# Adding expert blocks' low halves by an identity product, one-step one-hots, and all low splits on DVE

## The reference

```python
q = (h @ w_q).reshape(T, 8, 256)                      # 8 heads
s1 = einsum('thd,kd->thk', q[..., :128], k1)          # 128 keys
s2 = einsum('thd,kd->thk', q[..., 128:], k2)
v1, i1 = top_k(s1, 16)
v2, i2 = top_k(s2, 16)
cand = v1[..., :, None] + v2[..., None, :]            # 256 candidates
top, pos = top_k(cand, 16)
idx = (i1 * 128 + i2) at pos                          # of 16384 experts
g = softmax(top)
act = gelu(einsum('thkd,td->thk', u_tab[idx], h)) * g
out = einsum('thk,thkd->td', act, v_tab[idx])
```

## Time and profile before

| | |
|---|---|
| median of 3 runs | 2080.0 us (2078.1 to 2082.48) |
| the profiled execution | 2074.85 us |
| its span, first to last instruction | 2073.1 us |
| mean granted TensorE clock | 0.973 |
| UP, MID, ROUTE, DOWN begin at about | 584, 775, 975, 1385 us |

### The profile page before, as it was taken

One profiled execution on the slowest core, in us unless ns is written; L12 is line 12 of the kernel. 1 busy time (PEld: TensorE's weight loads), 2 busy tenths in 40 slices (PEclk: granted clock), 3 DMA queues, 4 the chain that ended last, 5 costly groups with the idle time before them and its releaser, 6 DMA issues.

```text
span 2073.1 us, 30937 instructions
## 1 busy us (share of the span) xinstructions
PE 1853.7 (89%) x9774; PEld 1575.1 (76%) x9774; DVE 1656.0 (80%) x2537; ACT 901.2 (43%) x1399; POOL 379.9 (18%) x281
## 2 busy tenths in 40 slices
PE   4999999898999997888889888978999999999997
PEld 4888886337988886777888888876677777777675
DVE  4668887666888999999988888857777777777786
ACT  3011233106455443444666666654444444444444
POOL 0000000000013243333444344421101010101010
PEclk9999999998999999999999999999999999999999
DMA  9997665996966668777888888888898989898885
GB/s 359 422 421 268 223 233 194 395 404 243 335 229 211 211 220 305 246 240 251 307 310 311 310 311 298 304 289 322 309 338 314 338 314 333 313 335 319 325 313 204
DMA packets 135958, 618.04 MB, mean 298 GB/s; under 512 B 16049, under 2 KB 24785, under 8 KB 99025
## 3 DMA queue, kind: packets, MB, share of 16 engines
q1 hardware_dynamic: 105984, 464.57, 61.8%
q0 software_dynamic: 18496, 134.24, 17.5%
q10 hardware_dynamic: 11410, 18.36, 2.4%
HBM read 600.26 MB, written 16.79 MB: 298 GB/s over the span
## 4 chain that ended last, share of the span: by engine, by line
DVE 20%; PE 15%; DMA 15%; issue 13%; ACT 5%; POOL 1%; DVEq 1%; SPq 1%; ACTq 1%; POOLq 0%
DMA raw<-in_peer_v 11%; DVE w_lo L379 7%; PE ps L1346 5%; PE ps L998 4%; PE ps L1007 3%; ACT w_hi L720 3%; DMA raw<-in_peer_u 2%; DVE oh L1387 2%; DVE big L1427 2%; DVE big L1863 2%; PE ps L1299 1%; POOL w_lo L379 1%; DVE big L1763 1%; ACT oh L839 1%; DMA big<-in_peer_v,row_ix 1%
## 5 line engine op out<-in xcount | busy, mean ns | idle before, releaser
L720 ACT ACTIVATE w_hi<-raw 128x1024 fp32r<-128x1024 f32 x544 | 574.5, 1058 | 641.9 <-DMA raw<-in_peer_v 143.4
L379 DVE TENSOR_TENSOR w_lo<-raw,w_hi 128x1024 fp32r<-128x1024 f32 x476 | 595.5, 1257 | 231.6 <-ACT w_hi L720 209.6
L998 PE MATMUL ps<-a,w_hi 128*128 128x384 f32 x2048 | 428.0, 352 | 6.2 <-ACT w_hi L720 5.4
L1346 PE MATMUL ps<-w_hi,a 128*128 128x512 f32 x1536 | 397.2, 394 | 24.6 <-ACT w_hi L720 18.8
L998 PEld LDWEIGHTS ps<-a,w_hi 128*128 128x128 f32 x2048 | 363.8, 197 | 7.7 <-issue 6.3
L1346 PEld LDWEIGHTS ps<-w_hi,a 128*128 128x128 f32 x1536 | 286.6, 189 | 99.1 <-ACT w_hi L720 32.6
L1007 PE MATMUL ps<-a,w_lo 128*128 128x192 f32 x2048 | 286.3, 282 | 58.1 <-DVE w_lo L379 41.3
L1007 PEld LDWEIGHTS ps<-a,w_lo 128*128 128x128 f32 x2048 | 274.2, 198 | 79.4 <-DVE w_lo L379 58.5
L1346 PE MATMUL ps<-w_lo,a 128*128 128x512 f32 x1024 | 283.6, 399 | 35.2 <-DVE w_lo L379 35.1
L379 POOL TENSOR_TENSOR w_lo<-raw,w_hi 128x512 fp32r<-128x512 f32 x136 | 217.5, 1621 | 409.0 <-ACT w_hi L720 378.1
L1346 PEld LDWEIGHTS ps<-w_lo,a 128*128 128x128 f32 x1024 | 188.5, 189 | 97.9 <-DVE w_lo L379 61.0
(11 more groups left out here) (227 smaller groups left out, 1803.1 us busy)
## 6 DMA issues: line engine op xcount, KB each, us to landing
raw<-in_peer_u SPq DMA_DIRECT2D x256, 512.0 KB
raw<-in_peer_v SPq DMA_DIRECT2D x256, 512.0 KB
early<-in_w_ada SPq DMA_DIRECT2D x60, 1024.0 KB, 10.4
early<-in_w_front SPq DMA_DIRECT2D x42, 1024.0 KB, 9.5
raw<-in_w_ada SPq DMA_DIRECT2D x20, 1024.0 KB, 10.0
raw<-in_peer_wq SPq DMA_DIRECT2D x32, 512.0 KB
big<-in_w_gate_f SPq DMA_DIRECT2D x16, 1024.0 KB, 5.5
raw<-in_w_front SPq DMA_DIRECT2D x14, 1024.0 KB, 8.7
```

Of the source, the lines that this page charges most:

```text
L379: engine.tensor_tensor(w_lo[:, s % 2, part], ring[j % ph.ring][:, part], w_hi[:, s % 2, part].bitcast(F32), ALU.subtract)\
L720: act.activation(w_hi[:, s % 2, :], ring[j % ph.ring], ACT.Copy).then_inc(hi_ready, 1)
L998: done = pe.matmul(ps[:, b % 2, 0:2 * TD].rearrange("p (m t) -> p m t", m=2), w_hi[:, half, k * P:(k + 1) * P], a_pair[:, kc, :, 0:TD], st ...
L1346: done = pe.matmul(ps[:, 4 * tt + 2 * (j % 2) + n, :], a, w[:, j % 2, n * 512:(n + 1) * 512], start=i is None and blk == 0 and w is w_hi a ...
```

## The change

Columns 0 to 191 and the low half are added by PE: ACT copies the low half into a new fp32r tile `low`, and PE multiplies it by an fp32r identity into the same columns of the bank, between the two units of the next block (`add_low`). `add_block` is gone from DVE. ACT takes the gelu straight from PSUM into `stage`, and PE uses the bank again after the gelu.

A mask group is made by DVE alone: one compare for the four plain one-hots and, for each token, one instruction with two scalar operands that compares and multiplies by the gate. ACT's scaling is gone. Two of the six groups of an iteration (all of them in ROUTE's first) are made a unit earlier.

All units are of kind "w": DVE makes every low part and POOL none. The pairs of 256-column pick instructions become single instructions of 512 columns. At DOWN's start the first sums of rows begin at unit 6 and not before unit 2; the small matrix `pair` takes over the space of `sel_T` and is made there.

```diff
 PH_WQ = Phase(None, BLOCKS // 4, "wwwwwwww")
-PH_UP = Phase(PH_WQ, EXPERT_BLOCKS // 32, "wwwp" * 4)
-PH_MID = Phase(PH_UP, EXPERT_BLOCKS // 32, "wwpwwpwwpwwpwwpw")
-PH_ROUTE = Phase(PH_MID, EXPERT_BLOCKS // 16, "wwwp" * 4)
+PH_UP = Phase(PH_WQ, EXPERT_BLOCKS // 32, "w" * 16)
+PH_MID = Phase(PH_UP, EXPERT_BLOCKS // 32, "w" * 16)
+PH_ROUTE = Phase(PH_MID, EXPERT_BLOCKS // 16, "w" * 16)
 PH_DOWN = Phase(PH_ROUTE, EXPERT_BLOCKS // 8, "w" * 16)
...
 ROWS = PEER_HEADS * TOPK // SLICES
-USE_FIRST, MASK_FIRST, PUT_FIRST = (5, 7, 9, 11, 13, 15), (5, 7, 9, 11, 13, 15), (7, 9, 11, 13, 15, 15)
-USE, MASK, PUT = (1, 4, 6, 9, 12, 14), (0, 3, 6, 8, 11, 14), (3, 6, 8, 11, 14, 15)
+USE_FIRST, MASK_FIRST, PUT_FIRST = (5, 7, 9, 11, 13, 15), (4, 6, 8, 10, 12, 14), (7, 9, 11, 13, 15, 15)
+USE, MASK, PUT = (1, 4, 6, 9, 12, 14), (0, 3, 5, 8, 11, 13), (3, 6, 8, 11, 14, 15)
 DOTS_MID_FIRST, DOTS_MID = tuple(range(6, 16)), (1, 4, 6, 9, 12, 14)
...
 assert ROW_ROUTE + N_ROUTE * (PH_ROUTE.n - 1) == ROWS and N_MID % 3 == 0 and N_ROUTE % 3 == 0
-SUMS_AT = (0, 2, 4, 6, 8, 10, 12, 14)
+SUMS_FIRST, SUMS_AT = (6, 8, 9, 10, 12, 13, 14, 15), (0, 2, 4, 6, 8, 10, 12, 14)
...
         dots_now = sb("dots_now", [P, N_ROUTE_FIRST, 2])
-        pair = sb("pair", [P, TD])
+        pair = sel_T[:, 0, :]
+        low = sb("low", [P, TD], F32R)
+        ident_r = sb("ident_r", [P, P], F32R)
...
+            act.activation(ident_r[:, :], ident[:, :], ACT.Copy).then_inc(ident_put, 1)
             wq_hi(KC)
...
+                act.wait_ge(split_used, at(i, 2 * per, 2 * b0 + 2))
+                act.activation(low[:, :], ps[:, b0 % 2, TD:2 * TD], ACT.Copy).then_inc(low_put, 1)
+
+            def gelu(b0, i, per):
+
                 b = b0 - B_UP
-                act.wait_ge(split_used, at(i, 2 * per, 2 * b0 + 2))
+                act.wait_ge(summed, at(i, per, b + 1))
                 if b % 2 == 0 and (b >= 4 or i is not None):
                     act.wait_ge(gel_out[b // 2 % 2], at(i, 4 * per, 16 * (b // 4)))
-                act.activation(stage[:, b % 4, :], ps[:, b0 % 2, TD:2 * TD], ACT.Copy).then_inc(low_put, 1)
-
-            def gelu(b0, i, per):
-
-                b = b0 - B_UP
-                act.wait_ge(summed, at(i, per, b + 1))
-                act.activation(stage[:, b % 4, :], stage[:, b % 4, :], ACT.Gelu).then_inc(gemm_evac, 1)
+                act.activation(stage[:, b % 4, :], ps[:, b0 % 2, 0:TD], ACT.Gelu).then_inc(gemm_evac, 1)
...
-            def scale_masks(g, i):
-
-                act.wait_ge(oh_masked, at(i, 6, g + 1))
-                for t in range(4):
-                    token = bass.ds(at(i, 24, 4 * g + t), 1)
-                    done = act.activation(masks[:, 1, t, :], masks[:, 1, t, :], ACT.Copy, scale=sel_T[:, 2, token])
-                done.then_inc(oh_ready, 1)
-
             def put_weights(g, i):
...
-            def route(j, i, mask_at, put_at):
+            def route(j, i, put_at):
                 for g in range(6):
-                    if mask_at[g] == j:
-                        scale_masks(g, i)
                     if put_at[g] == j:
...
                     act.wait_ge(row_gate_in, 16 * SLICES)
-                route(j, None, MASK_FIRST, PUT_FIRST)
+                route(j, None, PUT_FIRST)
             with act.Fori(1, PH_ROUTE.n) as i:
...
                     up_unit(PH_ROUTE, j, i)
-                    route(j, i, MASK, PUT)
+                    route(j, i, PUT)
...
         def _(pe):
+            def add_low(b, i, per):
+
+                pe.wait_ge(low_put, at(i, per, b - B_UP + 1))
+                pe.matmul(ps[:, b % 2, 0:TD], ident_r[:, :], low[:, :], start=False, stop=True,
+                          skip_group_check=True).then_inc(summed, 1)
+
             def product(ph, n, i, ahead=None):
...
                 else:
-                    pe.wait_ge(summed, at(i, ph.s_per // 2, b - 1 - B_UP))
+                    pe.wait_ge(gemm_evac, at(i, ph.s_per // 2, b - 1))
                 for half in range(2):
+                    if half and (b > B_UP or i is not None):
+                        add_low(b - 1, i, ph.s_per // 2)
                     place = ph.halves(n)[half]
...
                         done = pe.matmul(ps[:, b % 2, 0:TD], w_lo[:, half, k * P:(k + 1) * P], a_hi[:, kc, 0:TD],
-                                         start=False, stop=kc == KC - 1, skip_group_check=True)
+                                         start=False, stop=False, skip_group_check=True)
...
+            pe.wait_ge(ident_put, 1)
             for n in range(PH_UP.s_per // 2):
...
             pe.wait_ge(w_evac, TOKEN_GROUPS)
-            pe.wait_ge(summed, EXPERT_BLOCKS)
+            add_low(B_END - 1, None, 1)
+            pe.wait_ge(gemm_evac, B_END)
             down(None)
...
                     dve.wait_ge(oh_used, at(i, 6, g))
-                dve.tensor_tensor(masks, iota[:, None, None, :].to_broadcast([P, 2, 4, P]),
-                                  sel_T[:, 0:2, bass.ds(at(i, 24, 4 * g), 4)].unsqueeze(3).to_broadcast([P, 2, 4, P]),
-                                  ALU.is_equal).then_inc(oh_masked, 1)
+                dve.tensor_tensor(masks[:, 0], iota[:, None, :].to_broadcast([P, 4, P]),
+                                  sel_T[:, 0, bass.ds(at(i, 24, 4 * g), 4)].unsqueeze(2).to_broadcast([P, 4, P]),
+                                  ALU.is_equal)
+                for t in range(4):
+                    token = bass.ds(at(i, 24, 4 * g + t), 1)
+                    done = dve.tensor_scalar(masks[:, 1, t, :], iota[:, :], sel_T[:, 1, token], sel_T[:, 2, token],
+                                             ALU.is_equal, ALU.mult)
+                done.then_inc(oh_ready, 1)
...
                     low_part(dve, ph, j, i)
-                if ph in (PH_UP, PH_MID, PH_ROUTE):
-                    m = j // 2
-                    if j % 2 and (m or i is not None or ph is not PH_UP):
-                        add_block(ph.block - B_UP + m - 1, i, ph.s_per // 2)
                 if ph is PH_MID:
...
                     dots_at(j, i, DOTS_ROUTE if i is not None else DOTS_ROUTE_FIRST, ROW_ROUTE, 6)
-
-            def add_block(b, i, per):
-
-                dve.wait_ge(low_put, at(i, per, b + 1))
-                dve.tensor_tensor(stage[:, b % 4, :], ps[:, b % 2, 0:TD], stage[:, b % 4, :], ALU.add)\
-                    .then_inc(summed, 1)
...
                 lo(ph, j0 + 6, i)
-                cols = iota[:, None, 0:TOPK].to_broadcast([P, TOPK, TOPK])
-                for which, pick in enumerate((pick_a, pick_b)):
-                    d = dve.tensor_tensor(pick, pos_f[:, which, :].unsqueeze(2).to_broadcast([P, TOPK, TOPK]),
-                                          cols, ALU.is_equal)
-                chain(d)
+                chain(dve.tensor_tensor(picks, pos_f.unsqueeze(3).to_broadcast([P, 2, TOPK, TOPK]),
+                                        iota[:, None, None, 0:TOPK].to_broadcast([P, 2, TOPK, TOPK]), ALU.is_equal))
                 lo(ph, j0 + 7, i)
-                for which, pick in enumerate((pick_a, pick_b)):
-                    d = dve.tensor_tensor(pick, pick, ix16f[:, which, None, :].to_broadcast([P, TOPK, TOPK]),
-                                          ALU.mult)
-                chain(d)
-                for pick, dst in ((pick_a, idx1), (pick_b, idx2)):
-                    d = dve.tensor_reduce(dst[:, bass.ds(r, 1), :].rearrange("p o n -> p (o n)"), pick, AXX,
-                                          ALU.add)
-                chain(d)
+                chain(dve.tensor_tensor(picks, picks, ix16f[:, :, None, :].to_broadcast([P, 2, TOPK, TOPK]),
+                                        ALU.mult))
+                chain(dve.tensor_reduce(idx[:, :, bass.ds(r, 1), :].rearrange("p m o n -> p m (o n)"), picks, AXX,
+                                        ALU.add))
                 assert step[0] == CHAIN_STEPS
...
             dve.tensor_copy(expert_u, expert_f.rearrange("p h k -> p (h k)")).then_inc(expert_made, 1)
-            dve.memset(pair[:, 0:TS], 0.0).then_inc(pair_made, 1)
-            dve.memset(pair[:, P:TD], 0.0).then_inc(pair_made, 1)
-            dve.tensor_tensor(pair[:, TS:P], ident[:, 0:TS], ident[:, TS:P], ALU.add).then_inc(pair_made, 1)
             all_experts(PH_MID, PEER_HEADS)
...
                         lo(PH_DOWN, j, i)
-                    if j in SUMS_AT and (i is not None or j >= 4):
-                        add_row(SUMS_AT.index(j), i)
+                    sums_at = SUMS_AT if i is not None else SUMS_FIRST
+                    if j in sums_at:
+                        add_row(sums_at.index(j), i)
...
                 lo(PH_DOWN, j, None)
-            add_block(EXPERT_BLOCKS - 1, None, 1)
             dve.wait_ge(w_evac, TOKEN_GROUPS)
+            dve.memset(pair[:, 0:TS], 0.0).then_inc(pair_made, 1)
+            dve.memset(pair[:, P:TD], 0.0).then_inc(pair_made, 1)
+            dve.tensor_tensor(pair[:, TS:P], ident[:, 0:TS], ident[:, TS:P], ALU.add).then_inc(pair_made, 1)
```

(23 more changed lines are left out.)

## The result

The changed kernel takes **1986.7 us**, the median of four runs (1985.42 to 1988.32), against 2079.69 for the kernel before on the same chip (2078.1 to 2082.48): a ratio of 0.955, 95% interval 0.9535 to 0.9568.

A forecast was written before the change was run, and what follows sets the result against it. DVE, stretched by POOL's splits, bounds UP and MID; no engine fills ROUTE; transfers bound DOWN. Savings 11.5 (UP) + 16 (MID) + 24 (ROUTE) + 4 (DOWN's start) = 56 us, 2080 - 56 = 2024 us, range 2010 to 2038.

The forecast's parts named there:

- The mechanism: In UP, MID and ROUTE, DVE instructions meeting a POOL split stand still about as long as POOL works; moving splits ends this.
- ROUTE's term: ROUTE: transfers at DOWN's share need 47.8 us an iteration; 47.0 taken, 3 us saved in each of eight, 24 us.
- TensorE's bound of 44.8: ROUTE: PE's units 36.6, one-hot products 51.3/7 and identity products 0.9 sum to 44.8 us an iteration.
- the rival at 2006: ROUTE falls to PE's 44.8 us and DOWN's start gives all 7: 74 us saved, 2006 us; chance 0.18.
- DVE's side of ROUTE: ROUTE: DVE needs 41.6 us an iteration from splits, dots and six mask groups of 1.4, at most 2.2, us each.
- TensorE's granted clock: Read as 0.99 in one ROUTE window and 0.93 in MID's, where PE waits more; no time saving was assigned.
- DOWN's start: Later first row sums free two splits queued behind the 12.66 us fetch wait: between 0 and 7.0 us saved, 4 taken.
- UP and the first MID: UP saves 3.5 us in three iterations, 1 in the first, 11.5 in all; MID's first, waiting for rows, saves 3.
- No fetch was locked out: Feared in ROUTE: DVE's one-hots keep POOL from writing fetch descriptors; ROUTE at 50 or over, 2048 to 2058 us; chance 0.03.
- the change doesn't do what it says: POOL's splits are not what stretches DVE: UP 45.2, MID 53.9 us, +16 with DOWN's 4, 2096 us; chance 0.04.
- the low half's round trip: PE waits mid-block for ScalarE's copy and the gelu, up to 1.24 us a block: +22, 2102 us; chance 0.05.
- transfers holding ROUTE at 0.86: Transfers limit ROUTE at that share, no gain there: 32 us saved, 2048 us; chance 0.18.

The follow-up runs named there:

- pool_reads: Changed kernel plus POOL subtracting two 512-column pieces read from SBUF after every fourth unit of UP and MID; ratio 0.9803 to the kernel before, UP 45.4 us.
- pool_writes: Changed kernel plus POOL filling the same 512 columns with zeros, reading nothing, after every fourth unit of UP and MID; ratio 0.9564 to the kernel before, UP 38.8 us.
- undo_pool: Changed kernel with a quarter of the low splits back on POOL; ratio 0.9771 to the kernel before, UP 37.7, MID 47.2, ROUTE 47.7 us.
- only_allw: Kernel before with only POOL's 68 half splits moved to DVE; ratio 0.9791 to the kernel before, UP 41.4, MID 47.5, ROUTE 47.8 us.
- half_before: Kernel before with each ROUTE unit load moving 512 of its 1024 columns; ratio 0.9981 to the kernel before, ROUTE 50.0 us.
- half_loads: Changed kernel with each ROUTE unit load moving 512 of its 1024 columns; ratio 0.9519 to the kernel before, ROUTE 42.8 us.
- undo_sums: Changed kernel with DOWN's first row sums back before its units 2 and 3; ratio 0.9583 to the kernel before, DOWN 674 us.

## Why the prediction was wrong in its size

**The mechanism was right.** POOL's splits stretch DVE's two-input work and go with it (pool_reads, pool_writes, undo_pool). UP came to 38.8 (39.7 said) and MID to 46.07 in the window (46.4 said); the adds were worth 8 x 0.27 where DVE is the bound; the identity product costs 0.11 in the stream. In UP it held only to a degree: the move of POOL's splits was worth 1.7 us an iteration by itself (only_allw, 43.1 to 41.4), and with all else in place it costs 1.0 (undo_pool).

**The step that failed is ROUTE's term**, "DMA at DOWN's share 50 x 0.86/0.90 = 47.8 ... so I take 47.0". It took the share that another stage reached as a ceiling. DOWN's 0.90 is not the most that the queues give: the new ROUTE runs at 0.96 to 0.98. And ROUTE's 0.86 was what the old ROUTE asked for (half_before: no faster with 222 GB/s). At a share of 1, as an estimate from the earlier trace rows, the same transfers need 50 x 0.86 = 43.0 us an iteration; the changed kernel takes 43.7.

In bytes, ROUTE's traffic is 50 x 302 = 15.1 MB an iteration. The Trainium skill (SBUF — State Buffer, "A bandwidth-pool intuition that's wrong (but worth ruling out)") gives about 358 GB/s from HBM to one core; by that figure, as an estimate, the bound would have been 15.1 MB / 358 = 42.2. The traces do not bear it out as a limit: ROUTE itself reaches 363, and two of the 40 slices of the changed kernel's page, early in the run, reach 417 and 422:

```profile
GB/s 349 417 422 302 218 243 218 320 394 280 302 332 194 235 240 312 284 266 276 302 354 350 357 347 359 350 326 338 320 331 314 337 318 331 330 302 334 321 322 197
```

So a rate reached elsewhere is no measure of ROUTE's transfers either; their own share is.

**TensorE's bound of 44.8 was also too high**, which the rival at 2006 rested on. I added the one-hot products' busy time, 51.3/7 = 7.3 us, to a stream. But a product's modelled time overlaps the next one's. PE's timeline after:

```profile
1129.10 0.28 PE L975 MATMUL ps<-low,ident_r 128*128 128x192 f32 x1
1129.21 1.07 PE L1298 MATMUL ps<-oh 128*128 128x128 f32 x8
...
1130.05 0.77 PE L996 MATMUL ps<-a,w_hi 128*128 128x384 f32 x3
```

From 1129.21 to 1130.05 a group of eight takes 0.84 in the stream; six take 5.0. So the floor is 36.6 + 5.0 + 0.9 = 42.5, and half_loads measured 42.8. For the identity products I had taken the stream's 0.109, and these rows show just that (1129.10 to 1129.21); the one-hot products beside them I had not.

**DVE's side of ROUTE** came out as said: a mask group takes 1.63 us from 1124.60 to 1126.23 (0.68 for the compare, 1.11 for four one-hots), inside the 1.4 to 2.2 given, and DVE's 42.1 of 43.7 does not decide.

```profile
1124.60 0.68 DVE L1387 TENSOR_TENSOR oh<-iota,sel_T 128x512 f32<-128x512 f32 x1
...
1125.20 1.11 DVE L1392 TENSOR_SCALAR oh<-iota,sel_T 128x128 f32<-128x128 f32 x4
...
1126.23 1.22 DVE L379 TENSOR_TENSOR w_lo<-raw,w_hi 128x1024 fp32r<-128x1024 f32 x1
```

**ROUTE's parts don't add.** Of 6.5 us an iteration, POOL's splits are worth 2.4 where they go first (50.2 to 47.8, only_allw) and 4.0 where they go last (47.7 to 43.7, undo_pool); masks and adds together are worth 2.5 with the collisions (50.2 to 47.7) and 4.1 without (47.8 to 43.7), and each alone, undone last, 1.9 and 0.5. The chain's merged steps and the earlier masks were not tried alone.

**A term that the forecast put at nothing is TensorE's granted clock.** In the kernel before it was 0.91 over MID's three later iterations and 0.96 over ROUTE's seven, so part of that time ran at 1.2 GHz; in the changed kernel it is 1.00 in both. The forecast had read 0.99 from one ROUTE window. Shortly before six of the nine falls of the clock in that ROUTE stage TensorE had stood for 2.1 to 2.9 us. In only_allw ROUTE's clock is 0.97: its two iterations at 1.00 took 46.4 and 46.0 us, about the 46.1 expected, and the one at 0.91 took 51.1. So part of ROUTE's 6.5 us, and of what does not add up above, may be the clock's. No run separates it, and none shows whether the iterations were long because the clock fell, or the clock fell because TensorE stood in long ones.

**DOWN's start** gave about its term, for another reason: not the later sums (undo_sums, nothing lost) but the fetch, which no longer stands behind POOL's splits. I had read the wait of 12.66 us without asking when its fetch was issued. Either cure seems to be enough: in undo_pool, where POOL's splits stay and the fetch is late, the sums come later (DOWN 676).

**UP and the first MID** gave 7.5 us more than their terms. UP's first iteration saved 2.4 where I took 1, and each later one 4.3 where I took 3.5. For the first MID I took 3 because it waits for its first rows. That wait was 1.6 us before and is 2.92 in the changed kernel, so it gave no reason for the lower figure; which part of the 6.8 us is whose was not tested.

**The other rivals.** No fetch was locked out: a fetch takes POOL 1367 ns in ROUTE against 1452 before, and the one-hots 355 ns. That the change doesn't do what it says and that the low half's round trip makes it slower are both refuted above; transfers holding ROUTE at 0.86 is refuted by half_before.

## What to carry to other kernels

A share that the queues reach in one stage is not a ceiling for another; before a transfer bound goes into a sum, take the stage's own share up to 1, and look whether the stage ever waited for a transfer. Read the granted clock over the whole of a stage, not in one window of it. Add pipelined products by the distance between starts, not by busy time. And when a second engine helps a first one, count not what it takes over but what the first loses while both read: here POOL's four splits an iteration cost 4 us in ROUTE and paid 1 us in UP.
